# State-space projection with B and C ahead of x: their products in the layer, step sizes in two parts, three weight subtractions on GpSimd

## The reference

```python
proj = h @ w_in                                   # 1024 -> 2048 (z) + 3072 (xbc) + 32 (dt)
z, xbc, dt_raw = ...
xbc = silu(causal_dwconv(xbc, conv_w, conv_b))    # four taps along the tokens
xs, bm, cm = xbc[..., :2048], xbc[..., 2048:2560], xbc[..., 2560:]   # x, B, C
dt = softplus(dt_raw + dt_bias)
a_cs = cumsum(dt * -exp(a_log))                   # within chunks of 128 tokens
cb = einsum('bclgn,bcsgn->bcgls', cc, bc)         # C times B, per chunk and group
y_diag = einsum(cb * decay(a_cs), x * dt)         # decay: exp(a_cs[l] - a_cs[s]), causal
states = einsum(bc, exp(a_cs_end - a_cs), x * dt)
y = y_diag + y_off(states) + xs * d_skip
```

## Time and profile before

| what | us |
|---|---|
| three timed runs | 1379.92, 1376.66, 1382.22 (median 1379.92) |
| the profiled execution, its own time | 1387.18 |
| its span, first to last instruction | 1385.4 |
| TensorE busy (PE) | 1329.5 (96% of the span) |
| VectorE busy (DVE) | 992.7 (72%) |
| ScalarE busy (ACT) | 774.7 (56%) |
| GpSimd busy (POOL) | 116.5 (8%) |
| chain of waits | PE 88%, DVE 6%, ACT 2%, SyncE's queue 2%, issue 1%, DMA 1% |
| granted TensorE clock, mean | 0.979 |

### The profile page before, as it was taken

The page is one execution under the profiler, slowest core; times in us unless marked ns, Lnnn a source line. Parts: engine busy times, 40 slices in busy tenths (PEclk is TensorE's granted clock), DMA queues, the critical chain, the costliest instruction groups (busy, mean ns, idle before and its releaser), DMA issues.

```text
span 1385.4 us, 30051 instructions
## 1 busy us (share of the span) xinstructions
PE 1329.5 (96%) x12384; PEld 1267.8 (92%) x12384; DVE 992.7 (72%) x1636; ACT 774.7 (56%) x1353; POOL 116.5 (8%) x151
## 2 busy tenths in 40 slices
PE   5999999999999999999997999999999999999998
PEld 5998978989989999989995899999999888999986
DVE  4769898978876665575898868886565554877754
ACT  4596775549455443454669654444455554644443
POOL 2000100000002110000203001111000100122100
PEclk8999998999999999999999999999999998999999
DMA  7643620223545537645672355546664621555461
GB/s 226 195 140 123 191 86 27 70 68 118 183 153 183 183 122 232 189 132 182 199 213 75 121 175 164 183 150 208 190 183 166 196 65 57 188 183 182 163 212 66
DMA packets 197810, 212.70 MB, mean 154 GB/s; under 512 B 8972, under 2 KB 186924, under 8 KB 197564
## 3 DMA queue, kind: packets, MB, share of 16 engines
q1 hardware_dynamic: 195132, 201.46, 45.4%
q0 software_dynamic: 2464, 9.52, 2.3%
q10 hardware_dynamic: 96, 0.02, 0.0%
HBM read 209.33 MB, written 1.65 MB: 152 GB/s over the span
## 4 chain that ended last, share of the span: by engine, by line
PE 88%; DVE 6%; ACT 2%; SPq 2%; issue 1%; DMA 1%; DVEq 0%; ACTq 0%
PE pb L458 21%; PE pb L459 21%; PE pb L460 21%; PE pb L2405 2%; PE pb L2729 1%; PE pb L2730 1%; PE pb L2731 1%; PE pb L2244 1%; PE pb L2233 1%; SPq L610 1%; DVE w_lo L504 1%; PE pb L2349 1%; PE pb L2350 1%; PE pb L2351 1%; DVE pj L1670 1%
## 5 line engine op out<-in xcount | busy, mean ns | idle before, releaser
L504 DVE TENSOR_TENSOR w_lo<-raw,w_hi 128x1024 fp32r<-128x1024 f32 (+2 forms) x384 | 465.6, 1216 | 139.6 <-ACT w_hi L498 138.4
L498 ACT ACTIVATE w_hi<-raw 128x1024 fp32r<-128x1024 f32 (+2 forms) x384 | 396.6, 1041 | 301.1 <-PE pb L460 221.4
L458 PE MATMUL pb<-x_hi,w_hi 128*128 128x256 f32 x1856 | 529.6, 285 | 5.9 <-DVE x_lo L1427 3.5
L459 PE MATMUL pb<-x_lo,w_hi 128*128 128x256 f32 x1856 | 527.1, 284 | 0.0
L460 PE MATMUL pb<-x_hi,w_lo 128*128 128x256 f32 x1856 | 526.9, 284 | 0.0
L458 PEld LDWEIGHTS pb<-x_hi,w_hi 128*128 128x128 f32 x1856 | 358.2, 193 | 8.8 <-DVE w_lo L504 6.7
L459 PEld LDWEIGHTS pb<-x_lo,w_hi 128*128 128x128 f32 x1856 | 358.3, 193 | 0.2
L460 PEld LDWEIGHTS pb<-x_hi,w_lo 128*128 128x128 f32 x1856 | 358.2, 193 | 0.0
L753 POOL TENSOR_TENSOR sub<-sub,rstd 128x256 f32<-128x256 f32 x66 | 72.0, 1106 | 584.1 <-ACT sub L1146 584.1
L458 PE MATMUL pb<-act_hi,w_hi 128*128 128x256 f32 x392 | 111.1, 284 | 3.3 <-DVE w_lo L504 3.3
L460 PE MATMUL pb<-act_hi,w_lo 128*128 128x256 f32 x392 | 110.9, 283 | 0.0
(11 more groups left out here) (363 smaller groups left out, 2277.1 us busy)
## 6 DMA issues: line engine op xcount, KB each, us to landing
raw<-in_ffn_w_up_dram SPq DMA_DIRECT2D x55, 1024.0 KB, 5.1
raw<-in_w_in_dram SPq DMA_DIRECT2D x28, 1024.0 KB, 5.1
raw<-in_ssd_w_in_dram SPq DMA_DIRECT2D x20, 1024.0 KB, 5.3
raw<-in_ffn_w_down_dram SPq DMA_DIRECT2D x16, 1024.0 KB, 5.6
raw<-in_fox_w_in_dram SPq DMA_DIRECT2D x16, 1024.0 KB, 5.8
raw<-in_ffn_w_down_dram SPq DMA_DIRECT2D x16, 896.0 KB, 5.8
raw<-in_ffn_w_gate_dram SPq DMA_DIRECT2D x11, 1024.0 KB, 5.3
raw<-in_ssd_w_out_dram SPq DMA_DIRECT2D x8, 1024.0 KB, 5.2
```

The costliest lines, as they stand in the source:

```text
L458: pe.matmul(o, w_hi[m][:, k, :], hi[:, k0 + k, :], start=first and k == 0, stop=False)
L459: pe.matmul(o, w_hi[m][:, k, :], lo[:, k0 + k, :], start=False, stop=False)
L498: act.activation(piece(ly, u, w_hi[m], nk, m), raw_piece(ly, u, s, nk, m), ACT.Copy).then_inc(sem("w_hi_ready"), 1)
L504: dve.tensor_tensor(piece(ly, u, w_lo[m], nk, m), raw_piece(ly, u, s, nk, m), piece(ly, u, w_hi[m], nk, m).bitcast(F32), ALU.subtract).the ...
```

## The change

- The units of `ssd_xbc` come in the order B, C, x (XBC_ORDER = 4, 5, 0, 1, 2, 3). The layer is written out on all engines, with no hardware loop.
- The step sizes are made in two parts: the part up to exp and log at (0, 1), the part from dt on, with the scans and exponentials, at (0, 3).
- TensorE transposes the step sizes at (3, 0), makes the B and C products of chunk 0 and 1 behind (4, 0) and (4, 2), and transposes B behind (4, 3). VectorE copies the step sizes at (3, 1), applies the masks at (4, 1) and (4, 3), copies B at (5, 0), to another place.
- ScalarE makes the differences of rounds 0 to 3 at (4, 0), (4, 2), (5, 0) and (5, 2).
- The low halves of (3, 3), (4, 3) and (5, 3) are made by GpSimd behind its decay pieces. VectorE only counts them on; TensorE and SyncE wait for GpSimd's semaphore `low_ssd_xbc` as well.

```diff
-        layer("ssd_xbc", cols(a["ssd_w_in_2"][0], SSD_INNER), [KC] * 6)
+        XBC_ORDER, XBC_POOL = (4, 5, 0, 1, 2, 3), 3
+        xbc_cols = cols(a["ssd_w_in_2"][0], SSD_INNER)
+        layer("ssd_xbc", lambda u: xbc_cols(XBC_ORDER[u]), [KC] * 6)
...
-            pairs = (n - lead - 2) // 2 if n >= 6 and ly.k_split == 1 else 0
+            pairs = (n - lead - 2) // 2 if n >= 6 and ly.k_split == 1 and ly.name != "ssd_xbc" else 0
...
                     pe.wait_ge(sem("w_lo_ready"), ly.item0 + M_PER_UNIT * u + m + 1)
+                    if ly.name == "ssd_xbc" and u >= XBC_POOL and m == M_PER_UNIT - 1:
+                        pe.wait_ge(sem("low_ssd_xbc"), u - XBC_POOL + 1)
...
         def dve_rest(dve, ly, u, p, m):
+            if ly.name == "ssd_xbc" and u >= XBC_POOL and m == M_PER_UNIT - 1:
+
+                dve.wait_ge(sem("w_lo_ready"), ly.item0 + M_PER_UNIT * u + m)
+                dve.nop().then_inc(sem("w_lo_ready"), 1)
+                return
...
                             sp.wait_ge(sem(ly.free[half][u][0]), ly.free[half][u][1])
+                            if ly.free[half][u][3] > 0:
+                                sp.wait_ge(sem(f"low_{ly.free[half][u][2]}"), ly.free[half][u][3])
...
-            pool.wait_ge(sem("evac_done"), L["ssd_xbc"].evac1 + BANKS)
+            ly, m = L["ssd_xbc"], M_PER_UNIT - 1
+            for u in range(XBC_POOL, len(ly)):
+                pool.wait_ge(sem("w_hi_ready"), ly.item0 + M_PER_UNIT * u + m + 1)
+                pool.tensor_tensor(w_lo[m][:, :, :], raw[(ly.u0 + u) % 2][:, :, P * m:P * m + P], w_hi[m][:, :, :].bitcast(F32),
+                                   ALU.subtract).then_inc(sem("low_ssd_xbc"), 1)
+            pool.wait_ge(sem("evac_done"), ly.evac1 + BANKS)
...
             def xbc_hook(u, m):
-                if isinstance(u, int) and (u, m) == (0, 1):
-                    step_sizes()
-
-            def step_sizes():
+                if (u, m) == (0, 1):
+                    step_logs()
+                if (u, m) == (0, 3):
+                    step_decays()
+                if u >= 4 and m % 2 == 0:
+                    differences(2 * (u - 4) + m // 2)
+
+            def step_logs():
...
+            def step_decays():
                 act.wait_ge(sem("acs_ready"), 2)
                 act.activation(acs_exp, acs[:, P:T], ACT.Exp)
...
+            def differences(i):
+                c, hq = divmod(i, 8)
+                act.wait_ge(sem(f"decay_landed{i % 2}"), 16 * (i // 2 + 1))
+                if i == 0:
+                    act.wait_ge(sem("heads_ready"), 1)
+                for r in range(4):
+                    t, h = att[i % NATT][:, r, :], 4 * hq + r
+                    go(act.activation(t, t, ACT.Relu, scale=-1.0, bias=tok_heads[:, c, h:h + 1]))
...
             def step_sizes(u, m):        # VectorE
+                if (u, m) == (0, 3):
+                    dve.wait_ge(sem("log_ready"), 1)
+                    link(stt(dt, dt_z, 0.0, dt_e, ALU.max, ALU.add))
+                    ...
+                if (u, m) == (3, 1):
+                    dve.wait_ge(sem("heads_turned"), 1)
+                    link(dve.tensor_copy(tok_heads[:, :, :].rearrange("p a h -> p (a h)"), pb[4][:, 0:5 * SSD_HEADS]))
+                    dve.nop().then_inc(sem("heads_ready"), 1)
+                if (u, m) in ((4, 1), (4, 3)):
+                    c = m // 2
+                    dve.wait_ge(sem("cb_done"), c + 1)
+                    tt(cbm[:, c], pb[6 + c][:, :].rearrange("p (g l) -> p g l", l=P), ..., ALU.mult).then_inc(sem("cbm_ready"), 1)
+                if (u, m) == (5, 0):
+                    dve.wait_ge(sem("b_turned"), 1)
+                    dve.tensor_copy(b_tok.rearrange("p g n -> p (g n)"), pb[5][:, :]).then_inc(sem("b_tok_ready"), 1)
...
+            def early_products(u, m):    # TensorE
+                if (u, m) == (3, 0):
+                    pe.wait_ge(sem("da_ready"), 1)
+                    for i, src in enumerate((acs[:, 0:P], acs[:, P:T], dt[:, 0:P], dt[:, P:T], da_end)):
+                        ins = turn(pb[4][:, SSD_HEADS * i:SSD_HEADS * i + SSD_HEADS], src)
+                    ins.then_inc(sem("heads_turned"), 1)
+                if (u, m) in ((4, 0), (4, 2)):
+                    pe.wait_ge(sem("xbc_ready"), 8)
+                    for g in range(SSD_GROUPS):
+                        ins = mm(pb[6 + c][:, P * g:P * g + P], xbc[:, 16 + g, t], xbc[:, 20 + g, t], start=True, stop=True)
+                    ins.then_inc(sem("cb_done"), 1)
+                if (u, m) == (4, 3):
+                    for g in range(SSD_GROUPS):
+                        ins = turn(pb[5][:, P * g:P * g + P], xbc[:, 16 + g, 0:P])
+                    ins.then_inc(sem("b_turned"), 1)
+            pe_layer(pe, L["ssd_xbc"], x_hi, x_lo, "x_lo_ready", X_BASE[2], early_products)
...
+                if i == 0:               # TensorE, first of the 16 rounds
+                    pe.wait_ge(sem("xbc_ready"), SSD_XBC)
```

More of the change, by code:

```diff
@@ L339, in build @@
         unit, item, evac = 0, 0, 0
+        POOL_LOW = {}
+        POOL_LOW["ssd_xbc"] = lambda u, last: u - XBC_POOL + 1 if last == M_PER_UNIT else 0
         occupant, kept_by_k = [[None, None], [None, None]], [False, False]
@@ L349, in build @@
                     ly.free[half].append(occupant[s][1 if ly.by_k != kept_by_k[s] else half])
-                    occupant[s][half] = ("w_lo_ready", item + M_PER_UNIT // 2 * (half + 1))
+                    last = M_PER_UNIT // 2 * (half + 1)
+                    occupant[s][half] = ("w_lo_ready", item + last, ly.name, POOL_LOW[ly.name](u, last) if ly.name in POOL_LOW else 0)
                     if half:
@@ L1274, in _ @@
             for i in range(16):
[L1275 to L1282, removed]
+                if i >= 4:
+                    differences(i)
                 sync()
@@ L1942, in step_sizes @@
-                dve.wait_ge(sem("narrow_done"), 1)
-                dve.wait_ge(sem("small_loaded"), 16 * 12)
-                for h in range(2):
-                    go(dve.tensor_copy(d_skip[64 * h:64 * h + 64, :], d_rows[64 * h:64 * h + 64, h::2]))
-                link(tt(dt_z, pb[4][0:SSD_HEADS, 0:T], rstd[0:SSD_HEADS, :], ALU.mult))
-                link(ts(dt_z, dt_z, heads_col[:, 0:1], None, ALU.add))
-                stt(dt_e, dt_z, -1.0, dt_z, ALU.mult, ALU.max).then_inc(sem("abs_ready"), 1)
@@ L1949, in step_sizes @@
[L1949 to L1954 removed]
+                if (u, m) == (0, 1):
+                    dve.wait_ge(sem("narrow_done"), 1)
+                    dve.wait_ge(sem("small_loaded"), 16 * 12)
+                    for h in range(2):
+                        go(dve.tensor_copy(d_skip[64 * h:64 * h + 64, :], d_rows[64 * h:64 * h + 64, h::2]))
+                    link(tt(dt_z, pb[4][0:SSD_HEADS, 0:T], rstd[0:SSD_HEADS, :], ALU.mult))
+                    link(ts(dt_z, dt_z, heads_col[:, 0:1], None, ALU.add))
+                    stt(dt_e, dt_z, -1.0, dt_z, ALU.mult, ALU.max).then_inc(sem("abs_ready"), 1)
@@ new lines, in step_sizes @@
+                if (u, m) == (0, 3):
+                    dve.wait_ge(sem("log_ready"), 1)
+                    link(stt(dt, dt_z, 0.0, dt_e, ALU.max, ALU.add))
+                    link(ts(dt_z, dt, heads_col[:, 3:4], -1.0, ALU.mult, ALU.mult))
+                    for c in range(2):
+                        s = slice(c * P, c * P + P)
+                        dve.tensor_tensor_scan(acs[:, s], ones[0:SSD_HEADS, :], dt_z[:, s], 0.0, ALU.mult, ALU.add).then_inc(sem("acs_ready"), 1)
+                if (u, m) == (3, 1):
+                    dve.wait_ge(sem("heads_turned"), 1)
+                    link(dve.tensor_copy(tok_heads[:, :, :].rearrange("p a h -> p (a h)"), pb[4][:, 0:5 * SSD_HEADS]))
+                    dve.nop().then_inc(sem("heads_ready"), 1)
@@ L1974, in _ @@
             heads_x(0, 0)
-            for c in range(2):
-                dve.wait_ge(sem("cb_done"), c + 1)
-                tt(cbm[:, c], pb[6 + c][:, :].rearrange("p (g l) -> p g l", l=P),
-                   tri[:, :].unsqueeze(1).broadcast_to([P, SSD_GROUPS, P]), ALU.mult).then_inc(sem("cbm_ready"), 1)
-            dve.wait_ge(sem("b_turned"), 1)
-            dve.tensor_copy(b_tok.rearrange("p g n -> p (g n)"), pb[5][:, :]).then_inc(sem("b_tok_ready"), 1)
             dve.wait_ge(sem("cbm_ready"), 2)
@@ L2522, in _ @@
             narrow_product(dt_w, SSD_HEADS, 1)
-            pe_layer(pe, L["ssd_xbc"], x_hi, x_lo, "x_lo_ready", X_BASE[2])
-            pe.wait_ge(sem("da_ready"), 1)
-            for i, src in enumerate((acs[:, 0:P], acs[:, P:T], dt[:, 0:P], dt[:, P:T], da_end)):
-                ins = turn(pb[4][:, SSD_HEADS * i:SSD_HEADS * i + SSD_HEADS], src)
-            ins.then_inc(sem("heads_turned"), 1)
+            def early_products(u, m):
[5 more added lines that the diff above has]
+                if (u, m) in ((4, 0), (4, 2)):
+                    c = m // 2
+                    t = slice(P * c, P * c + P)
+                    pe.wait_ge(sem("xbc_ready"), 8)
```

(10 more changed lines are left out.)

39 lines of the change are left out of this document (12 added, 27 removed).

## The result

The changed kernel takes 1389.4 us (median of 7 runs), the kernel before 1381.6 in the same comparison; the medians differ by 7.8. One of the 7 runs took 4462.8 us; the ratio leaves it out: 1.0069, 95% interval 1.0048 to 1.0089. That is +9.5 us (6.6 to 12.3); +7.4 was forecast, with a chance of 0.42 for slower by over 0.5%.

The account below looks back on a forecast made before the run. TensorE was taken to bound the layer, VectorE close behind, and ScalarE and VectorE the part after it; 0.2 + 3.0 + 4.0 + 3.0 - 2.8 = +7.4 us on the median 1379.9 gave 1387.3, range 1377 to 1392.

Parts of the forecast that it names:

- Step sizes: First units of the layer: both old TensorE waits go, new ones of 1.4 us come at (1,3) and (2,2); +0.2 us.
- Products in the layer: Small transposes, B and C matmuls and B transposes in the layer now stand where TensorE is the bound; +3.0 us.
- GpSimd: Units 3 to 5: three subtractions break into VectorE's taps, TensorE waits ahead of (4,2) and (5,2); +4 us (0 to +6).
- rival 3: Stalls bring half clock on TensorE, or a slower GpSimd decay chain stalls (3,3) too; +10 to +12 us; chance 0.12.
- Differences: Units 4 and 5: four groups on ScalarE lengthen its chain of convolution starts; +3 us at the layer's end (0 to +4).
- Behind the last tap: Behind the layer: VectorE loses 2.55 us of work, ScalarE four groups of differences (5.1); -2.8 us (-1.8 to -4.2).
- The low clock: Right behind the layer: TensorE's low clock comes earlier, costs 0.5 to 1 us in the first products, spares a 1.4 wait.
- signs named in advance: What the profile after should show of TensorE's waits, VectorE's taps, the (5,3) convolution start, first exponential and last tap.
- the wait ahead of (4,2): In unit 4 TensorE waits for the low half of (4,2): 1.9 us forecast, over 1.5 as the sign.
- the convolution start of (5,3): At the layer's end it was to come over 2.5 us behind its evacuation.
- Rival 1: Units 3 to 5: GpSimd doesn't break into the taps and ScalarE keeps up; about +1 us, 1381; chance 0.28.
- rival 2: Layer's end was the bound and gets faster: old waits go, no lock, chain behind gains; -3.3 us, 1376.6; chance 0.15.

Follow-up runs that it names:

- experiment 5: Experiment 1 with the exponentials of the step sizes' second part on ScalarE at (1,0) instead of (0,3); ratio 0.9999 to the kernel before.
- experiment 10: Kernel before with only step sizes in two parts, their exponentials at (1,0) and the silus of unit 0 at (1,3); ratio 1.0001 to the kernel before.
- experiment 1: Changed kernel without its GpSimd blocks, VectorE making all low halves of the layer again; ratio 1.0015 to the kernel before.
- experiment 11: Kernel before plus three spare GpSimd subtractions, the first waiting for nothing and so right behind GpSimd's two DMA issues; ratio 1.0053 to the kernel before.
- experiment 2: Changed kernel with ScalarE's differences of rounds 0 to 3 back behind the layer, GpSimd blocks kept; ratio 1.0056 to the kernel before.
- experiment 3: Changed kernel without GpSimd's blocks and with all differences behind the layer; ratio 1.0005 to the kernel before.
- experiment 9: Experiment 5 with B and C products, B transposes, masks and B copy behind the layer, early differences of rounds 0 and 1 only, unit 0's silus at (1,3); ratio 0.9989.
- experiment 4: Changed kernel, but GpSimd starts each of its three blocks only once block (u,0) of the unit is evacuated; ratio 1.0020 to the kernel before.
- experiment 8: Kernel before plus three spare GpSimd memsets of 128x1024, which write and read nothing; ratio 0.9989 to the kernel before.

## Why the prediction was right

The sign, the size (+7.4 against +9.5) and the main mechanism held: GpSimd's subtractions break into VectorE's taps, and TensorE then waits. That the size came near is partly luck, since two terms were off in opposite directions: GpSimd cost over twice what was forecast, the differences half or less. By the steps, against +10.5 in the stage:

- **Step sizes: +0.2 forecast, +0.6.** The two new waits stand where they were put, ahead of (1,3) and (2,2), 1.42 and 1.30 us long by the block starts (1.4 and 1.4 forecast). A small one ahead of (1,2) came on top (0.3), since VectorE makes that low half behind the taps of (0,3). The reason given for the one ahead of (1,3), ScalarE's wait for the scans, was right (experiment 5). For the one ahead of (2,2), the table load, it was wrong (experiment 10).
- **Products in the layer: +3.0, measured 2.7.**
- **GpSimd: +4, measured 8.3** (stage, against experiment 1). This is the term that was most mis-sized. The duration was right (2.4 to 2.5 us; 2.6 taken), and so was the break into the taps. But (3,3) was said to cost no wait on TensorE, because GpSimd would be busy until behind the taps. GpSimd came free at 696.07, 42.8 us behind the layer's first matmul (43.3 forecast), half a microsecond early. More, its queued subtraction held the tap from 695.00 on, while by its record a DMA issue was still running (experiment 11), so the taps of (2,3) were hit, and 2.5 us came ahead of (3,2). And half clock behind the waits, 3.2 us, stood under rival 3 with a chance of 0.12; experiment 2, with waits of up to 2.1 at the same places, had none of it, so it doesn't follow from the waits alone. The waits ahead of (4,2) and (5,2) were smaller than forecast (1.1 for 1.9, 2.2 for 2.6). Ahead of (4,2) TensorE asked 4.2 us later than forecast, the low half came 3.4 later.
- **Differences: +3 at the layer's end, measured 0.8** in the changed kernel and 1.4 without GpSimd (experiment 1 against 3). Two things were off. ScalarE's chain from the start of (5,0) to that of (5,3) took 7.9 us (731.00 to 738.90 in the changed kernel) for 8.9 forecast: the forecast added the two groups to the old 6.4 and kept the 0.68 of idle time in it, which the groups fill. And the chain began 6.4 us ahead of the layer's end, where 5.0 were forecast: counted from the layer's first matmul it began 3 us later than forecast, but the layer ended 4.5 later. (The forecast's own sum is also 0.3 short: 730.2, 8.9 and a start of 0.6 make 739.7, not 739.4.)
- **Behind the last tap: -2.8, measured -2.7**, the right number for partly the wrong reason. I credited VectorE's 2.55 us of removed work. Experiments 3 and 9 show that this alone is worth 0 and that two early groups of differences give it all. The low clock came earlier, as forecast: 0.2 us behind the last tap, for 6.8 us, where it had come some 10 us behind it, for 3.4.

Of the signs named in advance, four came: no wait ahead of (3,3), taps of over 2 us beside GpSimd's subtractions of 2.4 to 2.5, the first exponential 2.4 us behind the last tap, and the last tap over 6 us later (13.2, for some 10.5 forecast). Two didn't: the wait ahead of (4,2) was 1.1 and not over 1.5, and the convolution start of (5,3) came 0.9 us behind the end of its evacuation, not over 2.5.

Rival 1 fell with the held taps, rival 2 with every block table. Part of rival 3 came true beside the forecast: its half clock, 3.2 us, is more than the 2.1 between +7.4 and +9.5, and the cheaper differences gave part of it back.

## What to carry to other kernels

GpSimd is no spare VectorE. Before a two-input operation is given to it, look at what VectorE runs at the moment it would start: if both read SBUF and VectorE's has two SBUF inputs, VectorE stands still for nearly the whole of GpSimd's longer time (2.1 of 2.5 us here, a tap of 2.62 for 0.48). A start tied to an instant in which VectorE reads PSUM or waits cost 0.1 us of the layer (experiment 4; the stage was still 1.5 longer than with no GpSimd block), and it has to be made so. And work moved from a gap into a part that TensorE bounds costs its full length; it pays only if the chain behind really ran through it, which one look at what the first late instruction waits for would have told (here, in the earlier trace rows, the second product waits for ScalarE's exponential, not for VectorE's masks).

## What was not expected of the hardware

- A GpSimd operation that stands in its queue right behind a DMA issue shuts VectorE out from before its recorded start: taps of 3.77, 3.57 and 3.49 us (changed kernel, experiments 2 and 11), begun 1.09, 0.88 and 0.79 ahead of it, against 2.62 or 2.63 in the nine cases where nothing stood ahead of it.
- The same kind of wait on TensorE is followed by 1.2 GHz or not: those of 2.27 and 2.02 us were in the changed kernel, for 3.4 us each; one of 2.1 us in experiment 2 at the same place was not, and none of 0.85 to 1.72 was.
- Far behind the stage, in the attention (1136 to 1167 us), the same program gets more or less half clock by chance. Windows, first and second the two profiles of the kernel before, then experiment 8, which does the same work there:
```profile
1136.40:1167.10 30.70, 28.95 (x160) 26.01 (x160) 14.32 (x25) 13.56 (x36) 0.00 (x0) 0.72 0.11 35
1136.40:1167.10 30.70, 28.90 (x180) 26.25 (x180) 14.89 (x27) 14.38 (x36) 0.00 (x0) 0.83 0.11 35
```
```profile
1136.40:1167.10 30.70, 26.69 (x208) 24.51 (x207) 16.38 (x30) 16.22 (x38) 0.00 (x0) 1.00 0.16 50
```
 Mean clock 0.72, 0.83 and 1.00; the time behind the stage was 607.5, 604.5 and 600.0 us. That is more than nearly every effect studied here, while the stage came to 122.48 us in all three: small changes of such a program are read from the stage, not from the span, and even there the half clock has to be looked up.
